# Weight-chunk splits, hidden-row waits and a gain-row load moved in a four-layer fp32 kernel on one core

## What is computed

```python
def first_block(x, p, ...):                      # DEPTH = 2
    h = rms_norm(x); proj = h @ w_in             # three attention branches a, b, c
    merged = sum(sigmoid(h @ w_branch_gate[c]) * (out[c] @ w_branch[c]) for c in "abc")
    x = x + merged @ w_out
    h = rms_norm(x)
    x = x + (silu(h @ w_ffn_gate) * (h @ w_ffn_up)) @ w_ffn_down      # D_FF = 2816
    x = x + sigmoid(rms_norm(x) @ w_ple_gate) * (p @ w_ple_proj)
```

```python
    for layer in range(DEPTH):
        hn = rms_norm(h, norm_mix[layer])
        mix = even_mixer(...) if layer % 2 == 0 else odd_mixer(...)   # state-space + mLSTM, or HGRN
        h = h + mix
        h = h + mem_cross_attention(rms_norm(h, norm_xattn[layer]), mem_n, ...)
        h = h + peer_ffn(rms_norm(h, norm_ffn[layer]), ...)           # 128 gathered experts a token
    return rms_norm(h, norm_final)
```

## Time and profile before

| | us |
|---|---|
| three runs | 3150.7, 3148.26, 3150.2 |
| median | 3150.2 |
| the profiled execution | 3150.51 |
| its span from first to last instruction | 3148.7 |
| PE busy | 2614.6 (83%) |
| DVE busy | 2114.4 (67%) |
| ACT busy | 1083.7 (34%) |
| mean granted TensorE clock | 0.932 |

### The profile page before, as it was taken

The page is one execution under the profiler, slowest core; times in us unless marked ns, Lnnn a source line. Parts: engine busy times, 40 slices in busy tenths (PEclk is TensorE's granted clock), DMA queues, the critical chain, the costliest instruction groups (busy, mean ns, idle before and its releaser), DMA issues. The chain is left out here.

```text
span 3148.7 us, 35828 instructions
## 1 busy us (share of the span) xinstructions
PE 2614.6 (83%) x13038; PEld 1901.5 (60%) x13038; DVE 2114.4 (67%) x4121; ACT 1083.7 (34%) x1939; POOL 597.5 (19%) x547
## 2 busy tenths in 40 slices
PE   8988999998899989899687666667999787766675
PEld 7957997795799788688553222225888553222222
DVE  6457664646765466454699888866664689888875
ACT  4345443435544356444222111113644221112111
POOL 0000000000000000000354444450000155444442
PEclk9989999999999989999898888888999899888888
DMA  6422543542254343244799999997434699999996
GB/s 254 166 88 81 178 174 127 213 162 92 94 178 174 126 162 133 81 156 159 291 427 423 427 426 427 427 427 316 151 108 166 237 414 422 427 426 426 426 427 283
DMA packets 112497, 810.83 MB, mean 258 GB/s; under 512 B 12736, under 2 KB 12736, under 8 KB 14272
## 3 DMA queue, kind: packets, MB, share of 16 engines
q0 software_dynamic: 73728, 536.90, 40.7%
q1 hardware_dynamic: 38592, 271.63, 24.1%
HBM read 807.44 MB, written 1.05 MB: 257 GB/s over the span
## 5 line engine op out<-in xcount | busy, mean ns | idle before, releaser
L3152 PE MATMUL ps<-arena 128*128 128x512 f32 x912 | 521.9, 723 | 270.4 <-ACT arena L3077 269.3
L162 DVE TENSOR_TENSOR ring_low<-ring,parts 128x2048 fp32r<-128x2048 f32 x218 | 496.7, 2291 | 352.6 <-ACT parts L155 349.6
L420 PE MATMUL ps<-parts,parts 128*128 128x256 f32 x2528 | 570.9, 283 | 13.5 <-DVE ring_low L162 10.1
L3152 PEld LDWEIGHTS ps<-arena 128*128 128x128 f32 x912 | 201.4, 230 | 577.8 <-ACT arena L3077 350.4
L155 ACT ACTIVATE parts<-ring 128x2048 fp32r<-128x2048 f32 x218 | 414.2, 1912 | 302.4 <-PE ps L428 123.8
L420 PE MATMUL ps<-parts,ring_low 128*128 128x256 f32 x1824 | 513.8, 282 | 0.0
L428 PE MATMUL ps<-parts,parts 128*128 128x512 f32 x1344 | 445.3, 401 | 28.7 <-DVE ring_low L162 18.4
L420 PEld LDWEIGHTS ps<-parts,parts 128*128 128x128 f32 x2528 | 429.1, 189 | 16.4 <-issue 10.8
L2940 POOL DMA_INDIRECT arena<-in_experts,stage_index x276 | 323.3, 1171 | 572.1 <-PE ps L3152 270.5
L3152 PE MATMUL ps<-ring,arena 128*128 128x512 f32 x616 | 315.2, 649 | 105.3 <-ACT arena L3077 102.8
L2962 DVE CUSTOM_DVE_ANT_0 arena<-arena 128x1024 f32<-128x1024 f32 x276 | 333.7, 1227 | 96.6 <-DMA arena<-in_experts,stage_index 93.9
(11 more groups left out here) (476 smaller groups left out, 2942.5 us busy)
## 6 DMA issues: line engine op xcount, KB each, us to landing
ring<-in_stream SPq DMA_DIRECT2D x249, 1024.0 KB, 4.8
arena<-in_experts,stage_index POOLq DMA_INDIRECT x276
ring<-in_experts,stage_index POOLq DMA_INDIRECT x236, 22.7
gain_row<-in_gain_rows SPq DMA_DIRECT2D x4, 512.0 KB, 5.7
arena<-in_mem SPq DMA_DIRECT2D x2, 1024.0 KB, 5.0
arena<-in_stream SPq DMA_DIRECT2D x2, 1024.0 KB, 7.7
par<-in_params SPq DMA_DIRECT2D x4, 386.0 KB, 3.0
x<-in_x SPq DMA_DIRECT2D x1, 1024.0 KB, 5.1
```

Of the source, the lines that this page charges most:

```text
L162: dve.tensor_tensor(k.ring_low[v % SLOTS], whole, self.high[:, c % self.HIGH_SLOTS, :].bitcast(F32), ALU.subtract).then_inc(self.ph.sem("c ...
L420: last = pe.matmul(self.ps[:, 2 * pair + f // 2, (f % 2) * T:(f % 2 + 1) * T], w[:, f * P:(f + 1) * P], x[:, k, :], start=(k == 0 and i == ...
L3152: last = pe.matmul(k.ps[:, bank + n, :], diag[:, s % ROWS, :], rows[row_of[s]][:, D + n * BLK:D + (n + 1) * BLK], start=(s % SLOTS_PER_TOK ...
```

## The change

Six edits. (a) `project`, SP: the gain row is issued after the first 10 chunk loads, before the 12 for the gates. (b) `down` in `back`: PE waits for piece n of the hidden rows just before block 2n of `down`'s first group, instead of for all 11 before the first. (c) `back`: the first `w_out` chunk is split ahead of the merging of half 0 on both engines; the second, on ACT between the two merged halves as before, on DVE ahead of `merged_low(1)`. (d) `back`: the third `ple_gate` chunk is split ahead of the norm's squares and statistics. (e) attend phases: the first chunk is split in four pieces of 512 columns, two, then four tiles of mixed rows, then two, then the remaining tiles; PE waits for each piece. (f) `odd_mixer`: the third `hgrn_v` chunk is split on ACT before it waits for `to_end`, on DVE ahead of the decayed keys; the `keep_busy` at the end has 18 instead of 24. The core of the diff:

```diff
@@ class Split
+    def quarters_high(self, act, quarters):
+        for i in quarters:
+            if i == 0:
+                self.k.wait_chunk(act, self.first)
+            whole = self.k.ring[:, self.first % SLOTS, :]
+            act.activation(self.high[:, 0, self.quarter(i)], whole[:, self.quarter(i)], ACT.Copy
+                           ).then_inc(self.ph.sem("chunk_high" if i == CHUNK_BLOCKS - 1 else "quarter_high"), 1)
+        self.done["high"] = self.first + 1
+    def quarters_low(self, dve, quarters):
+        for i in quarters:
+            if i < CHUNK_BLOCKS - 1:
+                dve.wait_ge(self.ph.sem("quarter_high"), i + 1)
+            else:
+                dve.wait_ge(self.ph.sem("chunk_high"), 1)
+            cols, slot = self.quarter(i), self.first % SLOTS
+            dve.tensor_tensor(self.k.ring_low[slot][:, cols], self.k.ring[:, slot, cols], self.high[:, 0, cols].bitcast(F32), ALU.subtract
+                              ).then_inc(self.ph.sem("chunk_split" if i == CHUNK_BLOCKS - 1 else "quarter_split"), 1)
+        self.done["low"] = self.first + 1
+    def wait(self, pe, v, block):
+        i = block % CHUNK_BLOCKS
+        if self.quarters and v == self.first and i < CHUNK_BLOCKS - 1:
+            pe.wait_ge(self.ph.sem("quarter_split"), i + 1)
+        elif i == 0 or self.quarters and v == self.first:
+            pe.wait_ge(self.ph.sem("chunk_split"), v - self.first + 1)
@@ project_phase, SP
-                k.load_ahead(sp, ph)
+                k.load_ahead(sp, ph, end=gates.chunk0)
                 if k.layer == 0:
                     sp.dma_start(k.gain_row[:], k.dram["gain_rows"][0]).then_inc(ph.sem("gain_loaded"), 16)
+                k.load_ahead(sp, ph, gates.chunk0)
+                if k.layer == 0:
                     sp.wait_ge(ph.sem("gain_loaded"), 16)
@@ back_phase, PE
-                pe.wait_ge(ph.sem("hidden_low"), ffn_in.n)
+                def hidden_of(n):
+                    return lambda pe: pe.wait_ge(ph.sem("hidden_low"), n + 1)
                 k.linear_tok(pe, ph, down, (hidden_high, hidden_low), split=split, between={
+                    **{(0, 2 * n): hidden_of(n) for n in range(ffn_in.n)},
@@ back_phase, ACT
+                split.high_for(act, lins[2], 1, 1)
                 merged_high(0)
-                split.high_for(act, lins[2], 1, 1)
+                split.high_for(act, lins[2], 1, 2)
                 merged_high(1)
@@
                 gate_norm.make_high(act, 1)
+                split.high_for(act, gate, 0, 1)
                 gate_norm.squares(act)
@@ back_phase, DVE
-                        split.low_for(dve, lin, n, 2 if (i, n) < (2, 0) else 1)
+                        split.low_for(dve, lin, n, 2 if (i, n) < (2, 1) else 1)
@@
                             dve.sem_inc(ph.sem("merged_ready"), 1)
+                            if n == 1:
+                                split.low_for(dve, lin, 1, 2)
                             merged_low(n)
@@
                 gate_norm.make_low(dve, 1)
+                split.low_for(dve, gate, 0, 1)
                 gate_norm.statistics(dve, link)
@@ mixer_out, ACT (DVE the same with quarters_low and make_low)
-        split.first_high(act, 1)
-        mix.make_high(act)
+        split.quarters_high(act, range(0, 2))
+        mix.make_high(act, range(0, 4))
+        split.quarters_high(act, range(2, CHUNK_BLOCKS))
+        mix.make_high(act, range(4, 2 * mix.groups))
@@ odd_mixer_phase
-                k.keep_busy(pe, 2, 24)
+                k.keep_busy(pe, 2, 18)
                 act.activation(z.qT[:, 0:4, :], z.qT[:, 0:4, :], ACT.Silu).then_inc(ph.sem("q_silu"), 1)
+                split.high_for(act, lv, 0, 1)
                 act.wait_ge(ph.sem("to_end"), 1)
@@
                 dve.sem_inc(ph.sem("to_middle"), 1)
+                split.low_for(dve, lv, 0, 1)
                 dve.wait_ge(ph.sem("to_end_exp"), 1)
```

25 lines of the change are left out of this document (14 added, 11 removed).

## The result

| us | before | after |
|---|---|---|
| median of the runs made beside each other | 3150.45 (3148.26 to 3151.72, 4 runs) | 3109.12 (3107.13 to 3112.73, 4 runs) |
| the profiled execution | 3150.51 | 3108.5 |
| its span | 3148.7 | 3106.7 |
| mean granted TensorE clock | 0.932 | 0.935 |

The ratio is 0.9866, with a 95% interval of 0.9854 to 0.9878: 1.3% faster, 41.3 us between the medians where 42.4 were forecast. On another chip, later, the changed kernel gave 3110.64 (3107.88 to 3114.04) against 3150.82 for before (3145.37 to 3155.44, 9 runs), ratio 0.9869 (0.9854 to 0.9884).

A forecast was written before the change was run, and what follows sets the result against it. PE was taken as the bound in the weight-streaming stages, so a wait removed moves all that follows. Terms 6.8 + 10.5 + 7.8 + 7.6 + 3.9 + 4.0 + 1.8 = 42.4 us off 3150.5 give 3108; range 3100 to 3122.

The forecast's parts named there:

- (a): Start of `latent` in layer 0: earlier gain row saves 5.1 us of idle time and 1.7 of clock, 6.8 us.
- (b): Start of `down`: the 3.75 us wait for hidden rows goes, plus 1.5 of clock; two layers, 10.5 us.
- (c): At `w_out`: about 0.5 us of waiting before the second chunk replaces 2.36 and 0.53; 3.9 a layer, 7.8 us.
- (d): Third gate chunk: 2.2 us wait and 1.6 clock go in each layer, 7.6 us; fourth chunk's margin 0.1.
- (e): Attend phases, first chunk in quarters: 2.9 us in the odd layer, 1.0 in the even, 3.9 us.
- (f): Third value chunk, odd mixer: wait falls from 3.78 to 1.35 us, plus 1.6 of clock; 4.0 us.
- costs and gains nothing: In (c): DVE's order of the second `w_out` chunk's and merged half's low parts only moves an equal gap.
- (g): End of the odd mixer: with six fill calls fewer DVE ends last, next phase starts 1.8 us earlier.
- the low clock stays: Rival: low stretches fall elsewhere instead of vanishing, so the 11.2 us of clock are not gained; 3119, chance 0.17.
- new waits: Rival: thin margins fail at five places, 2.3 us each, some followed by cold clock; 3123, chance 0.09.
- The expert stages didn't absorb the gain: Rival: gathers, not PE's chain, set when expert stages start, so time stays near 3150; chance 0.03.
- the clock falls for working without a pause: Rival: in the streaming stages, about 1800 us, lost pauses lower the clock; at 0.96 it is 3180, chance 0.02.

The follow-up runs named there:

- the filled wait: Kernel before, its wait ahead of `down` kept but filled with matmuls on constants (8 calls in layer 0, 4 in layer 1): 3144.61 us.
- A third order: Changed kernel with the second `w_out` chunk's low part made on DVE before the last group of branch c: 3107.67 us.

## Why the prediction was right

The forecast was 3108 and the changed kernel took 3109.12. Step by step:

- (a), (b) and (f) came as worked out. A wait that stands alone between stretches in which PE works was worth its whole length, and nothing second in line was late: the third `down` chunk had the margin it was given (split by 457.95, PE at it at 459.75), the eleven new waits left no gap. For (a) and (b) this rests on the lined-up traces and on the filled wait, for (f) on the run with the chunk put back.
- (c) came to 3.8 and 3.5 us for 3.9 forecast, with 0.72 us of waiting where 0.5 stood: DVE's row of the merged half begins at 301.88, 5.2 us after PE began the chunk, and PE waits until it is through. The step "I take the same for layer 1", although layer 1 had no low clock there, was the right one, and the run with filled waits shows why: 7.68 us at either clock.
- The sentence in (c) that the order of the low parts "costs and gains nothing" is true for the order that it turned round, and says nothing of the chain itself. The 1.18 us in which DVE waits for ACT were there to be seen, and used, they give 0.7 us a layer. A third order costs 0.8 a layer.
- (d): the margin of 0.1 us at the fourth gate chunk, the thinnest of the sum, held with 0.14. Its low part starts at 525.69 and takes 2.29, so it is ready at 527.98, and PE needs it at 522.57 + 5.55 = 528.12, and doesn't wait. What is less sure is the clock term of 1.6 us a layer. In the two traces compared it is there in full, but with the waits back neither layer showed it. It came 3 times in 6, so as an expected value it is 0.8 a layer, and the sum would have been 40.8, some 3110, which the medians (3109.12 and 3110.64) don't tell from 3108. The prediction's own row of layer 1 of `w_out` had said so much: the same wait of 2.36 us with the clock at 1.00.
- (e): the odd layer was right to 0.3 us (start of the product 2.50 us into the phase, 1.02 us of waiting at the second chunk for 1.1). For the even layer the prediction chose 1.0 between 0, with the low clock handed on to the product, and 1.7, without it. Both ends occur: 0.3 to 0.7 in six traces, 1.7 in three. What it had wrong is the chain between: the last turns don't begin earlier but 0.5 us later than before, since they now stand behind two waits, and the gain comes from there being eight of them and not sixteen.
- (g) gave 1.6 to 1.7 for 1.8, as DVE's end comes 0.60 us before the new phase; the 0.41 of the earlier trace rows is counted from PE's own last matmul.
- The rival "the low clock stays" (3119) falls: it was at none of these places in the three traces of the changed kernel. The rival "new waits" (3123) falls as well: what waits remain are 0.72, 1.02 and 1.34 us, near the 0.5, 1.1 and 1.35 worked out. The expert stages didn't absorb the gain: the last took 3.0 us more than in before, no more than such a stage differs from trace to trace. That the clock falls for working without a pause shows nowhere; the mean clock rose from 0.932 to 0.935.
- What no step had: the low stretches outside the change (2.2 and 1.1 us gone or shorter, 1.6 new), 1.8 us at the start of the program, and the play of the last expert stage (3.0 us). They nearly cancel. A forecast of this kernel to 1 us is luck; the interval was asked to cover this and did.

One thing stays open: why a wait of 2.2 to 2.4 us is followed by the low clock in one case and not in the other. The idle time and the work on both sides are the same to 0.02 us, so they don't decide it. That the outcome in the even mixer goes with the length of an earlier low stretch, four times and eight times, points to the moment at which the wait comes; no run tested this.

## What to carry to other kernels

Where one engine streams and the others prepare its operands, list each wait of the streaming engine with what stands in front of its releaser: a preparation that can be made early, but is queued behind work that has time, can be moved ahead of it at no cost, and the gain is the whole wait as long as the next operand has a margin. Work out that margin with the durations of the rows, since 0.1 us was enough here; and look for the engine's holes as well as its order, because a step that is too early on one engine (the low part ahead of its high part) costs more than it was to save. Count the clock behind a wait fully where the wait is long (2.84 us and more inside a phase here), and by half where it is about 2.2 to 2.4. And don't read a few us between single runs as the effect of an edit, when chance stretches at low clock and the gathered stages move the time by as much.

## What the runs showed of the hardware that was not expected

- The low clock behind PE's waits of 2.19 to 2.39 us came 15 times in 34, at the same place with the same wait both ways; behind 2.84 us and more, inside a phase, 10 times in 10, and behind the 6.59 at `latent` 2 in 2; behind lone waits of 1.3 to 1.9 us never. Three starts of phases, with 2.62, 2.79 and 3.46 us, gave 2, 11 and 9 of 12, so the length of the wait alone doesn't decide. With a wait of 3.75 us filled to 0.29 us by matmuls on constants, it didn't come.
- One low stretch of 3.4 us costs 1.2 to 1.7 us where PE works all through it (7.20 against 5.56 at the gate). It costs nothing where another engine sets the next start (`w_out`, 7.68 us at either clock) or where PE's next waits take it up (62.48 us in the even attend phase with and without it).
- The nine later runs of before spread over 3145.37 to 3155.44, 10 us. Low stretches have a part in such a spread, and so have the expert stages: over the twelve traces the same matmuls of the first took 638.9 to 644.0 us and those of the last 628.8 to 633.5. How large each part is in the spread of the runs was not measured.
